# Opening loads of a two-stack transformer kernel in quarters, and attention probabilities scaled before they are turned

## The reference, cut to what matters

```python
def hybrid_layer(x, ...):
    h = rmsnorm(x, norm_g)
    proj = h @ w_in                       # 14 blocks of 256 columns
    y_a = conformer_conv(a_u, a_v, ...) * silu(a_z)      # 31 taps, layernorm, silu
    y_b = short_gated_conv(b_b, b_c, b_x, ...) * silu(b_z)
    y_c = window_gqa(c_q, c_k, c_v, sink) * silu(c_z)
    y_d = neighborhood_attn(d_q, d_k, d_v, rpb) * silu(d_z)
    return x + concat(y_a, y_b, y_c, y_d) @ w_out

# both attentions, per head and block of 128 queries:
#   p = softmax(scores [, sink]);  o = p @ v
```

## Time and profile before

| | |
|---|---|
| median of 3 runs | 1271.8 us |
| profiled execution, its own time | 1271.64 us |
| its span (first to last instruction) | 1269.8 us |
| TensorE matmul busy | 1260.5 us, 99% |
| VectorE busy | 986.7 us, 78% |
| ScalarE busy | 697.5 us, 55% |
| GpSimd busy | 270.0 us, 21% |
| granted TensorE clock | 0.999 |

### The profile page before, as it was taken

The page is one execution under the profiler, slowest core; times in us unless marked ns, Lnnn a source line. Parts: engine busy times, 40 slices in busy tenths (PEclk is TensorE's granted clock), DMA queues, the critical chain, the costliest instruction groups (busy, mean ns, idle before and its releaser), DMA issues.

```text
span 1269.8 us, 21116 instructions
## 1 busy us (share of the span) xinstructions
PE 1260.5 (99%) x7986; PEld 1124.0 (89%) x7986; DVE 986.7 (78%) x1187; ACT 697.5 (55%) x929; POOL 270.0 (21%) x258
## 2 busy tenths in 40 slices
PE   9999999999999999999999999999999999999998
PEld 8998999888888899988888888888889998888886
DVE  6999789898767679868767778767676986877676
ACT  6674567465444586836444455444458673644444
POOL 2763275283000113201000009100011420100000
PEclk9999999999999999999999999999999999999999
DMA  9854654647666554346666655766654535566661
GB/s 281 257 183 166 202 147 150 180 146 222 198 189 187 156 165 144 128 141 185 196 184 185 198 166 176 214 182 190 198 161 138 166 134 150 177 189 197 193 186 52
DMA packets 281359, 224.02 MB, mean 176 GB/s; under 512 B 25996, under 2 KB 264234, under 8 KB 281288
## 3 DMA queue, kind: packets, MB, share of 16 engines
q1 hardware_dynamic: 279144, 220.23, 57.5%
q10 hardware_dynamic: 2032, 2.67, 0.6%
q0 software_dynamic: 112, 0.15, 0.0%
HBM read 221.85 MB, written 3.14 MB: 177 GB/s over the span
## 4 chain that ended last, share of the span: by engine, by line
PE 90%; DVE 6%; ACT 2%; issue 2%; DMA 0%; POOLq 0%; SPq 0%; DVEq 0%; POOL 0%; ACTq 0%
PE wide L1692 26%; PE wide L1695 13%; PE big L1659 9%; PE big L1660 9%; PE big L1661 8%; PE wide L1659 6%; PE wide L1660 6%; PE wide L1661 6%; DVE w_lo L936 2%; PE wide L1811 1%; PE big L1716 1%; PE big L1800 1%; PE big L1786 1%; DVE work L1345 1%; PE wide L1981 1%
## 5 line engine op out<-in xcount | busy, mean ns | idle before, releaser
L936 DVE TENSOR_TENSOR w_lo<-w_raw,w_hi 128x2048 fp32r<-128x2048 f32 x203 | 475.0, 2342 | 94.5 <-ACT w_hi L512 90.2
L512 ACT ACTIVATE w_hi<-w_raw 128x2048 fp32r<-128x2048 f32 x204 | 389.6, 1911 | 165.0 <-PE big L1661 125.2
L1692 PE MATMUL wide<-h_both,w_hi 128*128 128x512 f32 x1408 | 356.7, 393 | 0.0
L1692 PEld LDWEIGHTS wide<-h_both,w_hi 128*128 128x128 f32 x1408 | 254.6, 189 | 48.5 <-DVE h_both L951 2.0
L1659 PE MATMUL wide<-h_both,w_hi 128*128 128x256 f32 x736 | 213.6, 290 | 0.3 <-DVE h_both L951 0.3
L1660 PE MATMUL wide<-h_both,w_hi 128*128 128x256 f32 x736 | 208.1, 283 | 0.0
L1661 PE MATMUL wide<-h_both,w_lo 128*128 128x256 f32 x736 | 208.1, 283 | 0.0
L1695 PEld LDWEIGHTS wide<-h_both,w_lo 128*128 128x128 f32 x1408 | 194.2, 190 | 15.0
L1695 PE MATMUL wide<-h_both,w_lo 128*128 128x256 f32 x1408 | 198.8, 282 | 0.0
L1659 PE MATMUL big<-w_hi,y_hi 128*128 128x512 f32 x480 | 189.1, 394 | 0.0
L1660 PE MATMUL big<-w_lo,y_hi 128*128 128x512 f32 x480 | 187.3, 390 | 0.0
(11 more groups left out here) (254 smaller groups left out, 1459.1 us busy)
## 6 DMA issues: line engine op xcount, KB each, us to landing
w_raw<-in_w_in SPq DMA_DIRECT2D x112, 512.0 KB, 4.7
w_raw<-in_ffn_w_gate SPq DMA_DIRECT2D x88, 512.0 KB, 4.0
w_raw<-in_ffn_w_up SPq DMA_DIRECT2D x88, 512.0 KB, 5.2
w_raw<-in_ffn_w_down SPq DMA_DIRECT2D x88, 512.0 KB, 4.1
w_raw<-in_w_out SPq DMA_DIRECT2D x32, 512.0 KB, 4.3
work<-rpb_shifted SPq DMA_DIRECT2D x32, 64.0 KB, 3.4
rpb_shifted<-rpb_rows SPq DMA_DIRECT2D x10, 147.0 KB
x<-in_x SPq DMA_DIRECT2D x2, 512.0 KB, 6.6
```

Of the source, the lines that this page charges most:

```text
L512: nc.scalar.activation(w_hi[:, r, :], w_raw[:, r, :], ACT.Copy).then_inc(hi_ready, 1)
L936: v.tensor_tensor(w_lo[:, r, :], w_raw[:, r, :], w_hi[:, r, :].bitcast(F32), ALU.subtract).then_inc(lo_ready, 1)
L1692: t_.matmul(o, hi[:, kt, c], h_both[:, kt].rearrange("p a s -> p (a s)"), start=kt == 0, stop=False, skip_group_check=True)
```

## The change

1. **Loads.** The first parts are (slot, first tile, last tile): (0, 0-2), (0, 2-4), (1, 0-4), (0, 4-8), (1, 4-8), and x comes as tiles 0-2, 2-4, 4-8. SyncE's order: x 0-2, w part 0, x 2-4, w part 1, w part 2, x 4-8, w part 3, w part 4: 8 DMAs in place of 6, the same bytes. Identity and norm weights come as one tensor `front` in one DMA of ScalarE's queue.
2. **Opening order.** ScalarE and VectorE round part 0, then h of tiles 0-1, part 1, h of tiles 2-3, part 2, then as before. The multiplication of norm weights moves behind part 4. TensorE: 4 warm-up matmuls, the turn of tiles 0-1, 1 warm-up matmul, the turn of tiles 2-3; then part 0 (12 matmuls), part 1 with the turn of the right tiles of x between its halves (12), part 2 (24), then as before.
3. **Probabilities.** In the first stack heads 0 and 1 of a unit are scaled by VectorE in place (at the end of finish), heads 2 and 3 by ScalarE (normalize, at the head of step u + 8, ahead of the rounding of slot i + 3). turn_probs waits for both. spread_inverse and the multiplication of line 1144 go; aux is used 4 times a layer in place of 8.
4. **Order on VectorE.** finish(0) moves to the end of step 7 (behind the w_lo of slot 9), finish(1) and finish(2) to the end of steps 8 and 9 (behind the w_lo of slots 11 and 12), finish(3) to step 10, ahead of the w_lo of slot 13. The taps of steps 11 and 12 move to 10 and 11.

```diff
-WARM = (5, 2)
+WARM = (4, 1, 0)
+FIRST_PAIRS = [(0,), (1,), (2, 3)]
+FIRST_PARTS = [(0, 0, 2), (0, 2, 4), (1, 0, 4), (0, 4, 8), (1, 4, 8)]
-DVE_TAPS_AT = {2: 3, 3: 3, 4: 2, 5: 2, 6: 3, 11: 3, 12: 4}
+DVE_TAPS_AT = {2: 3, 3: 3, 4: 2, 5: 2, 6: 3, 10: 3, 11: 4}
...
-                weight_half(0, 0)
-                x_half(0)
-                weight_half(1, 0)
-                x_half(1)
-                weight_half(0, 1)
-                weight_half(1, 1)
+                x_part(0, 0, 2)
+                weight_part(0)
+                x_part(1, 2, 4)
+                weight_part(1)
+                weight_part(2)
+                x_part(2, 4, 8)
+                weight_part(3)
+                weight_part(4)
...
-            half_hi(0, 0)
-            act.wait_ge(gT_ready, 1)
-            round_h(0, (0, 1))
-            half_hi(1, 0)
-            for half in range(2):
-                act.wait_ge(x_in[half], 16)
+            part_hi(0)
+            act.wait_ge(front_in, 16)
+            round_h(0, (0,))
+            part_hi(1)
+            round_h(0, (1,))
+            part_hi(2)
+            for part in range(3):
+                act.wait_ge(x_in[part], 16)
             square(0)
             round_h(0, (2, 3))
...
+                    if SC_1 + 1 <= i < SC_1 + 5:
+                        normalize(un, i - SC_1 - 1, (2, 3))
                     round_hi(base, base3, i + RING)
...
                 link(v.reciprocal(row_inv[:, c:c + 4], row_sum[:, c:c + 4]))
                 dve.sem_inc(inv_ready, 1)
+                for h in heads:
+                    pr = probs[:, u % 2, h * S:(h + 1) * S]
+                    ins = v.tensor_scalar(pr, pr, row_inv[:, c + h:c + h + 1], None, ALU.mult)
+                    if h == heads[-1]:
+                        ins.then_inc(heads_scaled, 1)
...
-                    dve.wait_ge(aux_written, n + 1)
-                    v.scalar_tensor_tensor(out=scaled_gate, in0=aux[:, 0:2 * P]..., scalar=0.5,
-                                           in1=g[:, :, cols], op0=ALU.mult, op1=ALU.mult).then_inc(aux_read, 1)
-                    dve.wait_ge(aux_read, n + 2)
                     dve.wait_ge(mix_written, un + u + 2)
-                    v.tensor_tensor(yv, mix[:, 0:2 * P]..., scaled_gate, ALU.mult).then_inc(mix_read, 1)
+                    v.scalar_tensor_tensor(out=yv, in0=mix[:, 0:2 * P]..., scalar=0.5,
+                                           in1=g[:, :, cols], op0=ALU.mult, op1=ALU.mult).then_inc(mix_read, 1)
...
-                    if 0 <= u - 1 < 4:
-                        finish(un, u - 1, u - 1 < 2)
...
                     if i == 7:
                         split_lo(base, 6 + RING)
+                        finish(un, 0, True, (0, 1))
...
+                    if u == 3:
+                        finish(un, u, False, (0, 1))
                     if i != 6:
                         split_lo(base, i + RING)
+                    if u in (1, 2):
+                        finish(un, u, u < 2, (0, 1))
...
             def turn_probs(n, u, keys=S):
+                pe.wait_ge(probs_scaled, n + 1)
                 if n < DEPTH * 4:
-                    pe.wait_ge(probs_exp, n + 1)
-                else:
-                    pe.wait_ge(probs_scaled, n - DEPTH * 4 + 1)
+                    pe.wait_ge(heads_scaled, n + 1)
...
-                    if 0 <= u - 2 < 4:
-                        aux_free()
-                        spread_inverse(l * 4 + u - 2, u - 2, PLAIN if u - 2 < 2 else HORDER)
```

More of the change, by code:

```diff
@@ L203, in stacks_kernel @@
         rows = sb("rows", [P, 4, P])
-        gT = sb("gT", [P, GAINS * KT])
+        front = sb("front", [P, P + GAINS * KT])
         row_scale = sb("row_scale", [P, S])
@@ L268, in stacks_kernel @@
         pj_read = [sem("pj_read_even"), sem("pj_read_odd")]
-        x_in = [sem("x_in_left"), sem("x_in_right")]
-        ident_in, gains_in = sem("ident_in"), sem("gains_in")
+        x_in = [sem("x_in_first"), sem("x_in_second"), sem("x_in_right")]
+        front_in = sem("front_in")
         rows_in, table_in, swa_in, const_in = sem("rows_in"), sem("table_in"), sem("swa_in"), sem("const_in")
-        w_half = [sem(f"w_half_{i}{half}") for i in range(2) for half in "ab"]
+        w_part = [sem(f"w_part_{part}") for part in range(len(FIRST_PARTS))]
         first_hi, first_lo = sem("first_hi"), sem("first_lo")
@@ L576, in softmax_exp, with normalize @@
                 ins.then_inc(probs_exp, 1)
-            def normalize(un, u, keys):
+            def normalize(un, u, heads, keys=S):
                 act.wait_ge(inv_ready, un + u + 1)
                 c = 4 * (u % 2)
-                for h in range(NH):
+                for h in heads:
                     pr = probs[:, u % 2, h * S:h * S + keys]
@@ L630, in load_rest, with part_hi @@
                     act.dma_start(dst, src, allow_slow_non_contiguous=True).then_inc(const_in, 16)
[L632 to L640, removed]
+            def part_hi(part):
+                i, k0, k1 = FIRST_PARTS[part]
+                c = slice(k0 * G, k1 * G)
+                act.wait_ge(w_part[part], 16)
+                nc.scalar.activation(w_hi[:, i, c], w_raw[:, i, c], ACT.Copy).then_inc(hi_ready if part > 2 else first_hi, 1)
+            act.dma_start(front[:], a["front"]).then_inc(front_in, 16)
             act.wait_ge(warm, 1)
@@ L1009, in soft, with finish @@
                 ins.then_inc(probs_max, 1)
-            def finish(un, u, has_sink):
+            def finish(un, u, has_sink, heads=()):
                 c = 4 * (u % 2)
@@ L1044, in _, with part_lo @@
                 v.memset(cb_in[:, c, S + 1:S + 2], 0.0)
-            dve.wait_ge(gains_in, 16)
+            dve.sem_inc(aux_read, 1)
+            def part_lo(part):
+                i, k0, k1 = FIRST_PARTS[part]
+                c = slice(k0 * G, k1 * G)
+                dve.wait_ge(*((hi_ready, i + 1) if part > 2 else (first_hi, part + 1)))
+                v.tensor_tensor(w_lo[:, i, c], w_raw[:, i, c], w_hi[:, i, c].bitcast(F32),
+                                ALU.subtract).then_inc(lo_ready if part > 2 else first_lo, 1)
+            part_lo(0)
+            dve.wait_ge(front_in, 16)
+            split_h(0, (0,))
+            part_lo(1)
+            split_h(0, (1,))
+            part_lo(2)
+            for part in range(3):
+                dve.wait_ge(x_in[part], 16)
+            dve.sem_inc(x_block, 4)
+            split_h(0, (2, 3))
+            part_lo(3)
+            part_lo(4)
             g2 = slice(gain_row(DEPTH) * KT, (gain_row(DEPTH) + 1) * KT)
             v.tensor_tensor(gT[:, g2], gT[:, g2], gT[:, DEPTH * KT:(DEPTH + 1) * KT], ALU.mult).then_inc(gT_ready, 1)
[L1048 to L1065, removed]
+            dve.wait_ge(gT_ready, 1)
             split_lo(0, 2)
@@ L1709, in turn_x @@
             def turn_x(n, half):
-                pe.wait_ge(*((x_block, n * 4 + 2 * half + 2) if n else (x_in[half], 16)))
-                for pair in (2 * half, 2 * half + 1):
+                if n:
+                    pe.wait_ge(x_block, n * 4 + 2 * half + 2)
+                for pair in (2 * half, 2 * half + 1) if n else FIRST_PAIRS[half]:
+                    if not n:
+                        pe.wait_ge(x_in[half], 16)
                     for kt in (2 * pair, 2 * pair + 1):
@@ L1728, in first_slots, with some @@
             def first_slots(n, base, wide_sums=False):
[L1730 removed]
+                def some(i, kts, fresh, amid=None):
                     hi, lo = slot(i, KT)
@@ L1743, in some @@
                     return ins
-                for i in range(2):
-                    pe.wait_ge(*((lo_ready, base + i + 4) if n else (first_lo, i + 1)))
-                    for q in ((PJ_OF[n] - 2, PJ_OF[n] - 1) if n and i == 0 else ()):
+                for part, (i, k0, k1) in enumerate(() if n else FIRST_PARTS[:3]):
+                    pe.wait_ge(first_lo, part + 1)
+                    some(i, range(k0, k1), i == 0, (lambda: turn_x(n, 2)) if part == 1 else None)
+                for i in range(2) if n else ():
+                    pe.wait_ge(lo_ready, base + i + 4)
+                    for q in (PJ_OF[n] - 2, PJ_OF[n] - 1) if i == 0 else ():
                         pe.wait_ge(*evacuated(q))
-                    some(i, range(4), i == 0, i == 0 and n == 0)
-                    if i == 0 and n:
+                    some(i, range(4), i == 0)
+                    if i == 0:
                         turn_x(n, 1)
@@ L1813, in values @@
                 ins.then_inc(mix_written, 1)
[L1815 to L1823, removed]
             pe.sem_inc(slot_done, 3)
@@ L2119 @@
     given["gains"] = np.stack([np.asarray(w) for w in gains + [inputs["final_norm_2"]]])
-    given["gains_T"] = np.ascontiguousarray(given["gains"].reshape(GAINS * KT, P).T)
+    given["front"] = np.concatenate([np.eye(P, dtype=np.float32), given["gains"].reshape(GAINS * KT, P).T], axis=1)
     for to, names in (("params_1", ("conv_a_w", "conv_a_b", "ln_a_g", "ln_a_b", "conv_b_w")),
```

44 lines of the change are left out of this document (22 added, 22 removed).

## The result

| | before | after |
|---|---|---|
| median (us) | 1271.92 (8 runs, 1271.57 to 1273.4) | 1276.32 (8 runs, 1275.69 to 1278.8) |
| profiled execution (us) | 1271.64, span 1269.8 | 1278.8, span 1277.0 |
| PE, DVE busy (us) | 1260.5, 986.7 | 1259.7, 992.9 |

The ratio is 1.0033, 95% interval 1.0023 to 1.0043: slower by 4.4 us, where I had forecast 1270.8 and at most 1273.2. The profiled execution of after is the slowest of its eight, 2.5 us over the median, and DVE begins step 7 of layer 0 3.3 us later in it than before (61.64 for 58.32).

The account below looks back on a forecast made before the run. PE, busy 1260.5 of 1269.8 us, bounds the kernel; its 5.4 us saving is a ceiling. DVE lets through 0.3 us in layer 0 and 0.7 in layer 1: 1271.64 - 1.0 + 0.16 = 1270.8, range 1268.2 to 1273.2.

Parts of the forecast that it names:

- DVE's ledger: DVE's list per layer, step 7 to group a: +0.12 us in layer 0, -0.24 in layer 1; limits PE's gain.
- the turn of unit 2: First-stack attention: PE, running ahead, would wait 1.8 us there for DVE's inverse and ACT's pair of copies.
- ceiling of 4.7 for the attentions: Eight spreadings of inverse sums at 0.59 us each leave PE's list, 2.36 us a layer.
- The opening: First microseconds: first product near 7.3, PE gains 0.7 us at slot 0's right half, DVE follows 0.24.
- two more DMA issues: On SP, 0.56 us each: delay slot 2's fetch by 1.1 us, hidden behind a queue of 3 MB.
- Rival 3: Opening gives nothing: higher clock comes later, 24 products at 0.24 for 0.12 cost 2.9 us; 1271.1, chance 0.13.
- Come: eight scalings. I take 0.32: DVE's list, per layer: eight 128x256 scalings in SBUF at 0.32 us each, +2.56 us.
- Rival 2: Ends of steps 7 to 10: scalings meet POOL's adds at 0.73 each, 3.3 us more a layer; 1277.4, chance 0.12.
- The moves of finish and taps add and remove nothing on DVE: DVE's list, step 7 to group a: moves counted at no cost, changing only who waits.
- mostly takes over a wait that its neighbour had: Scalings beside POOL: POOL has no more adds than before, so 0.32 us each, nearer the undisturbed row.
- The waits: DVE's waits for PE close up, -0.64 in layer 0, -1.24 in layer 1; new wait for ACT +0.20.
- The forecast's best case: Scalings at 0.27 and no new wait give 2.0 us, the start's upper bound through DVE another 0.4: 1269.4.

Follow-up runs that it names:

- e6: The changed kernel with POOL's adds of the tap products and short convolution left out: 1267.42 us, ratio 0.9963 to the kernel before.
- e1: Only the new opening, with both first-stack attentions as in the kernel before: 1271.88 us, ratio 0.9999.
- e9: The changed kernel without DVE's eight scalings a layer, two heads of each unit staying unscaled: 1271.53 us, ratio 0.9994 to the kernel before.
- e2: Only the attention part of the change, with the opening of the kernel before: 1276.52 us, ratio 1.0036.
- e3: The changed kernel with its two groups of taps put back at steps 11 and 12: 1279.79 us, ratio 1.0063 to the kernel before.

## Why the prediction was wrong

**That DVE's ledger decides, with the two lags of 0.47 and 0.51 us: right.** The lag at the last slot is used up (0.05 us in layer 1) and PE got gaps ahead of turns and of the last slot. They are not where I had put the most: the turn of unit 2, for which I had worked out 1.8 us, waits 0.24 and nothing, that of unit 3 waits 1.10 and 0.68, with ACT as releaser, the last slot 0.24 and 0.28. The longest that both layers have (0.95 us, ahead of the turn back from the layer norm, behind DVE's L1206) and that ahead of slot 9 in layer 0 (1.03) I hadn't forecast. `e6` shows the other side: with DVE out of the way 4.1 us come through, of a ceiling of 4.7 for the attentions (8 x 0.59).

**The opening: right in its outcome, not in PE's part.** The opening of after:

```profile
7.80 0.36 PE L1674 MATMUL wide<-h_both,w_hi 128*128 128x256 f32 x1 [0.65 <-DVE h_both L960]
...
10.43 1.09 PE L1734 MATMUL big<-front,x 128*128 128x128 f32 x8 [0.18 <-DMA x<-in_x]
...
15.37 0.38 PE L1674 MATMUL wide<-h_both,w_hi 128*128 128x256 f32 x1 [0.25 <-DVE w_lo L1066]
```

The first product came at 7.80 (forecast 7.3, before 9.04). Slot 0's right half came at 15.37, 0.4 us earlier than before (15.78) where I had said 0.7: it waits for its w_lo, whose pair starts at 14.09 and not at 13.78. `e1` measures -0.1 us in the end, where I had given it 0.24. That two more DMA issues are hidden behind the queue was too sure: slot 6 came 1.7 us later on the mean, though no pair of runs shows a cost of it beyond the open 0.4. Rival 3's clock did not turn up: the products stand 0.12 us apart from 7.99 on.

**"Come: eight scalings. I take 0.32": mis-sized by where it stands.** 0.46 us each from start to start (3.69 / 8) in layer 1, and 0.27, my low end, in `e6` without POOL's adds. By unit (after, layer 1, DVE's timeline; the first row is the inverse ahead of unit 0's pair):

```profile
193.12 0.18 DVE L1025 RECIPROCAL small<-small 128x4 f32<-128x4 f32 x1
193.45 1.41 DVE L1029 TENSOR_SCALAR probs<-probs,small 128x256 f32<-128x256 f32 x2
...
204.58 1.38 DVE L1029 TENSOR_SCALAR probs<-probs,small 128x256 f32<-128x256 f32 x2
...
223.04 0.61 DVE L1029 TENSOR_SCALAR probs<-probs,small 128x256 f32<-128x256 f32 x2
```

The pairs of units 0 and 1 take 1.4 us, beside adds of POOL; those of units 2 (not shown) and 3 take 0.62 and 0.61, with POOL idle. Rival 2 named this, with 0.38 as the point at which the change is worth nothing. Its 0.73 each holds for two units of four. At 0.46 its sum gives 1273.0, so that its 1277.4 is close to the 1276.3 is luck: the moved steps, which it left out, make up most of the rest. In DVE's list 16 x 0.14 = 2.2 us of my error are this term. Taken out alone, though, the scalings are worth 4.8 us (`e9`), 0.30 each, close to my 0.32: what they occupy above that is place which waits and neighbours take otherwise.

**"The moves of finish and taps add and remove nothing on DVE": the step that failed.** Instructions were neither added nor removed, and I took that for "costs nothing". The runs showed a price in its place. In layer 1 all that is neither scaling, multiplication nor wait grew by 1.9 us: taps +3.21, row sums and inverses +1.21, casts and y_lo +0.85, against -1.65 and -1.57 for tanh copies and w_lo, and -0.18 for the rest. (In layer 0 of the same profile it grew by 0.9, the taps alone by 2.9.) The three taps of layer 1 where the change put them, at step 10, and POOL's rows beside them:

```profile
219.48 3.20 DVE L1147 SCALAR_TENSOR_TENSOR work<-work,parA_all 128x256 f32<-128x256 f32 x3
```

```profile
217.50 3.40 POOL L1571 TENSOR_TENSOR part_sum<-part_sum,fz 128x256 f32<-128x256 f32 x4 [5.58 <-ACT fz L602]
221.10 1.29 POOL L1590 TENSOR_TENSOR work<-proj 128x512 f32<-128x512 f32 x1 [0.20 <-POOL part_sum L1571]
```

POOL adds and multiplies nearly all the while, to 222.4. Before, the last four stood at step 12, and POOL had nothing to do from 225.4 until its next row:

```profile
226.06 2.05 DVE L1129 SCALAR_TENSOR_TENSOR work<-work,parA_all 128x256 f32<-128x256 f32 x4
```

```profile
228.33 2.82 POOL L1582 TENSOR_TENSOR work<-work,part_sum 128x256 f32<-128x256 f32 x1 [2.92 <-DVEq L1191]
```

My sentence that an inserted instruction "mostly takes over a wait that its neighbour had" is half right: w_lo and the tanh copies did become cheaper, by 3.2 us, but what was put in their place lost 5.3.

**The waits.** I counted -1.24 + 0.20 in layer 1; it was -1.44. The gaps for PE closed as forecast, another 0.69 us that DVE had waited behind its own inverses went too, and the new wait for ACT (0.49 us) came at unit 1, not at unit 3, where the taps cover it. The error of layer 1, 2.31 + 0.24 = 2.55 us, is then scalings 1.13, moved steps 1.86, waits -0.40, and the multiplications (-0.05). In layer 0 I had counted +0.36 from step 7 on and it was +1.97, an error of 1.61: scalings 1.26, moved steps 0.92, waits -0.52, multiplications -0.05. Together that is 4.2 of the 5.5 us by which the median missed, and the opening's 0.24 comes to it. The last 1.1 is not shown to belong to one cause. It may lie ahead of step 7 of layer 0: in `e2`, whose profile ran at its median, DVE began that step at 59.56, before at 58.32, with the same lists up to there; over the five profiles with the old opening it was 58.3 to 59.7. Why it varies stays open. (The forecast's best case has a slip as well: scalings at 0.27 and no new wait give 2.2 us by its own terms, not 2.0.)

## What to carry to other kernels

Two engines that hold each other up, as DVE and POOL do here, need one schedule: when an elementwise step is moved, lay the other engine's rows beside its new place before calling the move free. Price an inserted instruction beside the neighbour's work, not alone, then run the kernel once with that work taken out: it parts "more work" from "more meetings". And where an engine's list has been shortened, look at the lists of the two behind it; here a gain came only when ACT had the scalings and both lists were reordered to fit (1.5 of PE's 4.7 us).

## What the runs showed of the hardware

DVE and POOL hold each other up in both directions, but not in every instruction. In after, layer 1, the row sum's addition takes 0.69 us in the midst of POOL's adds and 0.16 at the end of one, as all four of both layers do in `e6` without adds, while the reciprocal right behind it takes 0.18 both times; one 128x256 add of POOL takes 2.81 us while w_lo holds DVE for 2.29:

```profile
192.40 0.69 DVE L1024 TENSOR_TENSOR small<-small 128x4 f32<-128x4 f32 x1
...
204.05 0.16 DVE L1024 TENSOR_TENSOR small<-small 128x4 f32<-128x4 f32 x1 [0.49 <-ACT small L579]
...
231.35 2.29 DVE L945 TENSOR_TENSOR w_lo<-w_raw,w_hi 128x2048 fp32r<-128x2048 f32 x1
```

```profile
231.43 2.81 POOL L1597 TENSOR_TENSOR work<-work,part_sum 128x256 f32<-128x256 f32 x1 [0.51 <-DVEq L1202]
```

The Trainium skill (SBUF — State Buffer, "Who interferes with whom") calls the shared ports an exclusive lock between DVE and GpSimd. By that rule each side waits for whole instructions of the other, and the trace agrees: 0.16 became 0.69 beside adds that take 0.74 alone. Had I let it into the sum as a matter of place and not of count, the moved taps would have stood there with a price.

In `e3`, layer 1, PE idled for 3.31 us at a granted clock of 1.00 and then went on at the clock's lower level, 1.2 GHz: six starts of 128x512 matmuls in a row stood 0.43 us apart in place of 0.23. Windows of `e3`:

```profile
236.00:238.20 2.20, 0.00 (x0) 0.00 (x0) 2.20 (x2) 0.00 (x0) 2.20 (x2) 1.00 0.01 4
238.20:242.00 3.80, 3.76 (x12) 3.17 (x13) 2.53 (x7) 0.63 (x1) 2.41 (x3) 0.55 0.87 244
242.00:246.00 4.00, 4.00 (x20) 3.25 (x19) 3.85 (x5) 1.29 (x1) 0.08 (x1) 1.00 0.18 49
```

The granted clock was 0.55 in the stretch behind the gap. In layer 0 an equal gap of 3.30 us, at 110 us, had no such tail (granted clock 1.00). Such a wait cost its length, and in one case of two 1.6 us more: from the transposes behind the gap to the seventh product behind them it took 3.44 us (238.24 to 241.68) for 1.86 in layer 0 (113.44 to 115.30).
